# Forty pairs of modulation columns: from products and sums on ScalarE and GpSimd to matrix multiplications on TensorE

## The chip, the cores and the metric

One core of a Trainium2 chip runs the whole kernel. The metric is the device time of one execution in microseconds (us). Three executions of the kernel before took 1823.52, 1839.77 and 1840.11 us, median 1839.77 us.

## The reference, cut to what matters

The model has two layers over 512 latent tokens and 256 context tokens of width 1024. Each layer takes six vectors of 1024 values (shift, scale and gate for the mixer and for the MLP) from one conditioning vector:

```python
s_lat = jax.nn.silu(c)[:, None, :]
for layer in range(DEPTH):                       # DEPTH = 2
    mod = jnp.split(s_lat @ mod_w[layer] + mod_b[layer], 6, axis=-1)   # mod_w: (2, 1024, 6144)
    h = modulate(rms_norm(x, norm_mix_pre[layer]), mod[0], mod[1])
    # mixer: layer 0 = DeltaNet + attention, layer 1 = short convolution
    x = x + mod[2] * rms_norm(y, norm_mix_post[layer])
    h = modulate(rms_norm(x, norm_ffn_pre[layer]), mod[3], mod[4])
    x = x + mod[5] * rms_norm(conv_ffn(h, ...), norm_ffn_post[layer])
```

The product of the vector with `mod_w` is a matrix-vector product with 2 x 6144 output columns. Only `mod[0]` and `mod[1]` of layer 0 are needed before the mixer; the other ten vectors are needed after the attention.

## The kernel before

**The data.** The conditioning vector lies as `cvec`, 128 partitions by 8 chunks (k). A "modulation pair" is a block of 256 columns of `mod_w`: 1 MB, laid in SBUF as 128 partitions by 8 chunks by 256 columns. There are 48 pairs. The first 8 are multiplied by TensorE at the start with `cvec` as the stationary operand (L543) and are not touched here. The 40 later ones, j = 0 to 39, go through six buffers `mod_raw_c` (`MSLOTS`) and end as 80 columns (128 values, one in each partition) in PSUM bank 7, from where VectorE adds the bias after the attention.

**The path of a later pair before.** SyncE's queue loads pair j when pair j-6 has been counted in `mod_done` (`load_mod_pair`, L357). ScalarE multiplies the eight chunks by the eight scalars of `cvec`, in place, eight activations (`products`, L1079, recorded as L1082). GpSimd adds the eight chunks in three halving steps, in place (`mod_half`, recorded as L1888). TensorE then sums over the partitions with two matrix multiplications for a pair: each takes 128 columns of the sum as the stationary operand and a single column of ones as the moving one (`mod_column`, L487).

**The order.** There is no planner: every engine runs its list in order, and semaphores tie them. The DeltaNet has six chunk steps s (`NT`) of seven levels l (`LEVELS`), two directions d in each, four heads. A level l >= 1 is: VectorE makes masked blocks `bl` (L1582); TensorE multiplies Z = bl x t (L689) for both directions; ScalarE copies Z out (`zs`, L1174); TensorE makes dT and dU (L710, L715); VectorE subtracts them into `tu` (L1593). At level 0 there is no Z; TensorE waits there for `bl` made by GpSimd and `bv` made by VectorE (L701, L704). Between the Z of both directions and the first dT stands the call `mod_columns(...)`, in every level, with the pairs that are due.

Pair j < 24 is due at level number `MOD_LEVEL[j]` = 7*(j//4) + 2*(j%4), so four pairs in seven levels: ScalarE at this number, GpSimd two and three levels later, TensorE four levels later. The other 16 pairs are due in the attention, which runs through 32 blocks i (8 heads by 4 query tiles): TensorE multiplies scores (L801, L802), transposes the probabilities of block i-2 (L775), multiplies a third of the values of an earlier head in three blocks of four (L786 to L788), then calls `mod_columns`. VectorE and ScalarE form the softmax and split each transposed block in a high and a low part. Pair j is due at block 7*(j-24)//4: ScalarE there, TensorE three blocks later, GpSimd in between.

fp32 matrix multiplications are recorded twice: one instruction in the code is two weight loads and two multiplications in the trace, here called passes. The 80 multiplications of L487 are 160 passes. Transposes, and the fp32r multiplications of split operands, are one pass.

Of the kernel before, what the change touches and what calls it, by code (L numbers as in the profile page):

```python
# [12 lines left out]
P = 128  # L13
# [39 lines left out]
def hybrid_trunk(nc, A, out):  # L53
    ctx = ExitStack()
    with ctx:
# [107 lines left out]
        def bank(b, n=512, o=0):  # L163
            return PS[:, b * 512 + o:b * 512 + o + n]
# [3 lines left out]
        def sem(name):  # L168
            if name not in sems:
                sems[name] = ctx.enter_context(nc.semaphore(name))  # L170
            return sems[name]
# [15 lines left out]

        PAIRS = MODS - 8
        DN_PAIRS = 24

        def acc_c(j):

            return 3 * (j + 1)

        def landed(j):

            return 16 * (j // MSLOTS + 1)
# [261 lines left out]
        def _(pe):  # L459
# [22 lines left out]
                        if k == KC - 1 and names[r]:  # L482
                            i.then_inc(sem(names[r]), 1)

            def mod_column(m, acc):

                mm(bank(7, 1, 16 + m), acc, ones[:, 0:1], start=True, stop=True).then_inc(sem("mod_done"), 1)  # L487

            def sum_columns(sq, idx, n, first, last):

                for j in range(n // P):
# [137 lines left out]
                item_rows(e)  # L629
            def mod_columns(pairs):  # L630
                for j in pairs:
                    pe.wait_ge(sem("mod_acc"), acc_c(j))
                    for part in range(2):
                        mod_column(16 + 2 * j + part, mraw_c[j % MSLOTS][:, 0, part * P:(part + 1) * P])

            def gate_rows(s):

# [12 lines left out]
            for s in range(NT):  # L650
# [30 lines left out]
                for l in range(LEVELS):  # L681
                    for d in range(2):
                        T, q = DT[d], (s * LEVELS + l) * 2 + d
                        if l == 0:
                            continue
                        pe.wait_ge(sem("Bl"), q + 1)
                        pe.wait_ge(sem("T"), q - 1)
                        for h in range(HEADS):
                            i = mm(bank(3 * d, P, h * P), T["bl"][:, h, :], T["tu"][:, h, :], start=True, stop=True)  # L689
                        i.then_inc(sem("Z"), 1)  # L690
                    mod_columns(mod_at(s * LEVELS + l, 4))
                    for d in range(2):
                        T, q, b0 = DT[d], (s * LEVELS + l) * 2 + d, 3 * d
                        if l == 0:
                            pe.wait_ge(sem("Bl"), q + 1)
                            pe.wait_ge(sem("TU0"), 2 * s + d + 1)
                            if CHUNK_ORDER[d][s] >= NTC:
                                pe.wait_ge(sem("egr"), 2 * s + d - 3)
                            pe.wait_ge(sem("bv"), 2 * s + d + 1)
                            for h in range(HEADS):  # L700
                                i = mm(bank(b0 + 1, P, h * P), T["bl"][:, h, :], T["tu"][:, h, :], start=True, stop=True)  # L701
                            i.then_inc(sem("dT"), 1)
                            for h in range(HEADS):
                                i = mm(bank(b0 + 2, P, h * P), T["tu"][:, 4 + h, :], T["bl"][:, h, :], start=True, stop=True)  # L704
                            i.then_inc(sem("dU"), 1)
                            continue
                        pe.wait_ge(sem("Zs"), z_count(s, l, d))
                        pe.wait_ge(sem("U"), u_count(s, l - 1, d))
                        for h in range(HEADS):
                            i = mm(bank(b0 + 1, P, h * P), T["tu"][:, 4 + h, :], T["zs"][:, h, :], start=True, stop=True)  # L710
                        i.then_inc(sem("dT"), 1)
                        if l == LEVELS - 1:
                            continue
                        for h in range(HEADS):
                            i = mm(bank(b0 + 2, P, h * P), T["zs"][:, h, :], T["tu"][:, 4 + h, :], start=True, stop=True)  # L715
                        i.then_inc(sem("dU"), 1)
                    if s == 0 and l < 6:
                        att_rows(l)
# [16 lines left out]
                for d in range(2):  # L735
# [9 lines left out]
                    for h in range(HEADS):  # L745
                        i = mm(bank(3 * d + 2, P, h * P), T["kd"][:, h, :], T["kbvn"][:, h, :], start=True, stop=True)
                    i.then_inc(sem("Sp"), 1)
            for q in range(LEVELS * NT, LEVELS * NT + 5):
                mod_columns(mod_at(q, 4))

            pe.wait_ge(sem("S"), 2 * NT)
            for n in range(NT):
# [41 lines left out]
            for i in range(A_HEADS * NQ + NQ + 1):  # L794
                if i < A_HEADS * NQ:
                    hh, qt = divmod(i, NQ)
                    t, half = hh % 4, hh // 4
                    r = slice(HD * half, HD * (half + 1))
                    pe.wait_ge(sem("expd"), cnt(i - 1))
                    b = 2 * (i % 2)  # L800
                    mm(bank(b), aq[r, t, qt * P:(qt + 1) * P], ak[r, 0:512], start=True, stop=True)  # L801
                    mm(bank(b + 1, CTX), aq[r, t, qt * P:(qt + 1) * P], ak[r, 512:768], start=True, stop=True).then_inc(sem("sc"), 1)  # L802
                if 2 <= i < A_HEADS * NQ + 2:
                    turn(i - 2)
                if i >= 6 and (i - 6) % NQ < 3:
                    values((i - 6) // NQ, (i - 6) % NQ)
                mod_columns(mod_block(i, 3))


            tcol = lambda r: (lambda w, k: w[slot[0]][:, k, r * P:(r + 1) * P])  # L810
# [228 lines left out]
        def _(act):  # L1039
# [36 lines left out]
            h_high(0, hc_hi, CTX, lambda c: modv[:, 0, c, 1:2])  # L1076
            h_high(1, h_hi, SEQ, lambda c: modv[:, 0, c, 0:1])

            def products(slot):  # L1079

                for k in range(KC):
                    i = nc.scalar.activation(slot[:, k, :], slot[:, k, :], ACT.Copy, scale=cvec[:, k, 0:1])  # L1082
                i.then_inc(sem("mod_prod"), 1)


            def square(e):
                t, n = items[e]
                if e >= 2:
# [74 lines left out]
            for s in range(NT):  # L1163
# [6 lines left out]
                for l in range(LEVELS):  # L1170
                    for d in range(2 if l else 0):
                        T = DT[d]
                        act.wait_ge(sem("Z"), z_count(s, l, d))
                        nc.scalar.activation(T["zs"][:, :, :].rearrange("p h t -> p (h t)"), bank(3 * d), ACT.Copy).then_inc(sem("Zs"), 1)  # L1174
                    for j in mod_at(s * LEVELS + l, 0):
                        act.wait_ge(sem(f"mod_in{j % MSLOTS}"), landed(j))
                        products(mraw_c[j % MSLOTS])
                for d in range(2):
                    T, k = DT[d], 2 * s + d
                    act.wait_ge(sem("WT"), k + 1)  # L1180
# [36 lines left out]
            for i in range(A_HEADS * NQ + NQ + 2):  # L1217
                if 2 <= i < A_HEADS * NQ + 2:
                    turn_hi(i - 2)
                if i < A_HEADS * NQ:  # L1220
                    act.wait_ge(sem("mx"), 2 * i + 2)
                    act.wait_ge(sem("Ptr"), cnt(i - 2))
                    nc.scalar.activation(prob[i % 3][:, :], bank(2 * (i % 2), ALL), ACT.Exp, scale=HD ** -0.5,
                                         bias=stat[:, 32 + i:33 + i], accum_out=stat[:, 64 + i:65 + i]).then_inc(sem("expd"), 1)
                if i >= 9 and (i - 9) % NQ == 0:
                    head_hi((i - 9) // NQ)
                for j in mod_block(i, 0):
                    act.wait_ge(sem(f"mod_in{j % MSLOTS}"), landed(j))
                    products(mraw_c[j % MSLOTS])
                if i == A_HEADS * NQ:  # L1230
                    act.wait_ge(sem("mod_done"), 2 * PAIRS)
                    split_hi(U_WOUT, 0)
                    split_hi(U_WOUT + 1, 1)
# [636 lines left out]
        def _(pool):  # L1870
# [10 lines left out]
                        i = G.tensor_tensor(t4[2][:, 0:n], t4[2][:, 0:n], t4[c % 2][:, 0:n], ALU.add)  # L1881
                    i.then_inc(sem("sqadd"), 1)

            def mod_add(n, dst, a, b):

                if n % 3:
                    pool.wait_ge(sem("mod_acc"), n)
                G.tensor_tensor(dst, a, b, ALU.add).then_inc(sem("mod_acc"), 1)  # L1888

            def mod_half(n, slot):  # L1890
                w = 4 >> (n % 3)
                mod_add(n, slot[:, 0:w, :], slot[:, 0:w, :], slot[:, w:2 * w, :])

            post_squares(0)
            post_squares(1)
            pool.wait_ge(sem("h"), KC)
            pool.wait_ge(sem("rope_in"), 32)

            def mod_parts(j, parts):
                pool.wait_ge(sem("mod_prod"), j + 1)  # L1900
                for part in parts:
                    mod_half(3 * j + part, mraw_c[j % MSLOTS])

            def mod_level(q):

                for lag, parts in ((3, (1, 2)), (2, (0,))):
                    for j in mod_at(q, lag):
                        mod_parts(j, parts)

            pool.wait_ge(sem("dn_ready"), 1)  # L1910
            for s in range(NT):
# [8 lines left out]
                for l in range(LEVELS):  # L1920
# [13 lines left out]
                    if s == 0 and 1 <= l < 6:  # L1934
                        pool.wait_ge(sem("shuf"), 2 * l - 1)
                        G.tensor_tensor(rope_tile(l - 1), rope_tile(l - 1), cosT[:, :], ALU.mult).then_inc(sem("rcos"), 1)
                    mod_level(s * LEVELS + l)
            for q in range(LEVELS * NT, LEVELS * NT + 4):
                mod_level(q)
            for j in range(DN_PAIRS, PAIRS):  # L1940
                mod_parts(j, (0, 1, 2))
            for j in range(4):
                for t in range(1, ACC):
                    pool.wait_ge(sem("ysq"), KC * j + t + 1)
# [50 lines left out]
```

## Time and profile before

| | us | share |
|---|---|---|
| profiled execution, own time | 1840.32 | |
| its span (first to last instruction) | 1838.2 | |
| TensorE multiplications busy | 1732.5 | 94% |
| TensorE weight loads busy | 1447.7 | 79% |
| VectorE busy | 984.0 | 54% |
| ScalarE busy | 704.0 | 38% |
| GpSimd busy | 324.2 | 18% |
| ScalarE's products (L1082, 320) | 131.7 | |
| GpSimd's sums (L1888, 120) | 189.4 | |

The DeltaNet levels run until 632 us of the span, the attention from 647 to 804 us, the rest (output projection, MLPs, short convolution) until the end. "PEclk" is the clock that TensorE was granted, as a share of 2.4 GHz; 0.50 is 1.2 GHz, its other level. A busy share of TensorE's multiplications counts overlapping records once and says little of how full it is; the starts of its weight loads (PEld), one behind the other, show how fast it goes.

### The profile page before, as it was taken

To read this page: it belongs to the slowest core of one execution; us is meant where nothing else is said; L and a number is where in the kernel's file an instruction comes from. 1 tells how busy PE (TensorE), PEld (TensorE's weight loads), DVE (VectorE), ACT (ScalarE), POOL (GpSimd) and SP (SyncE) were. 2 spreads that over 40 slices of the span, in tenths; PEclk is the share of its full clock that TensorE was granted. 3 is DMA by queue.
4 is the path that set the end of the run, shared out by engine and by line. 5 is a ranking of instruction groups with operands and counts; after the bars stand their busy time and mean duration, and the time that the engine had idled before them with its cause. 6 is when DMAs were issued, how large, how long until landed. Compare 5 with 4: busy or idle time off the path is not lost.

```text
span 1838.2 us, 22745 instructions
## 1 busy us (share of the span) xinstructions
PE 1732.5 (94%) x9143; PEld 1447.7 (79%) x9143; DVE 984.0 (54%) x1248; ACT 704.0 (38%) x1056; POOL 324.2 (18%) x227
## 2 busy tenths in 40 slices
PE   6899997989988999889999999999999999999998
PEld 3688887889988955657788888887888788888886
DVE  2633267777787565757644443446446744444222
ACT  2433433444444476834333332223223244433321
POOL 3000014543464345504000000110002100000000
PEclk9899998999999966989999999998999899999999
DMA  9213141212221323132232223230322122233221
GB/s 323 65 47 92 23 150 46 70 47 70 93 69 47 115 76 107 47 92 70 72 110 93 91 91 103 86 109 28 110 95 93 65 92 92 91 100 100 86 83 66
DMA packets 160942, 161.14 MB, mean 88 GB/s; under 512 B 11367, under 2 KB 159192, under 8 KB 160728
## 3 DMA queue, kind: packets, MB, share of 16 engines
q1 hardware_dynamic: 160856, 159.92, 27.4%
q8 instruction: 63, 1.03, 0.2%
q14 instruction: 23, 0.19, 0.0%
HBM read 157.81 MB, written 2.10 MB: 87 GB/s over the span
## 4 chain that ended last, share of the span: by engine, by line
PE 84%; DVE 8%; ACT 4%; issue 2%; POOL 1%; DMA 1%; SPq 0%; DVEq 0%; ACTq 0%; POOLq 0%
PE ps L467 17%; PE ps L468 17%; PE ps L469 17%; PE ps L710 3%; PE ps L689 3%; PE ps L715 3%; ACT mod_raw_c L1082 2%; PE ps L543 2%; PE ps L801 1%; PE ps L775 1%; PE ps L818 1%; PE ps L820 1%; PE ps L840 1%; PE ps L819 1%; DVE w_lo L1364 1%
## 5 line engine op out<-in xcount | busy, mean ns | idle before, releaser
L1364 DVE TENSOR_TENSOR w_lo<-w_raw,w_hi 128x2048 fp32r<-128x2048 f32 x100 | 229.0, 2291 | 513.9 <-ACT w_hi L1044 513.9
L467 PE MATMUL ps<-h_hi,w_hi 128*128 128x512 f32 x968 | 379.0, 392 | 0.4 <-DVE w_lo L1364 0.4
L468 PE MATMUL ps<-h_lo,w_hi 128*128 128x512 f32 x968 | 378.3, 391 | 0.0
L469 PE MATMUL ps<-h_hi,w_lo 128*128 128x512 f32 x968 | 377.9, 390 | 0.0
L1044 ACT ACTIVATE w_hi<-w_raw 128x2048 fp32r<-128x2048 f32 x100 | 191.1, 1913 | 337.7 <-PE ps L469 307.3
L1888 POOL TENSOR_TENSOR mod_raw_c<-mod_raw_c 128x1024 f32<-128x1024 f32 (+2 forms) x120 | 189.4, 1581 | 145.3 <-ACT mod_raw_c L1082 138.3
L467 PEld LDWEIGHTS ps<-h_hi,w_hi 128*128 128x128 f32 x968 | 182.5, 188 | 38.6 <-DVE w_lo L1364 0.8
L469 PEld LDWEIGHTS ps<-h_hi,w_lo 128*128 128x128 f32 x968 | 182.6, 189 | 38.0
L468 PEld LDWEIGHTS ps<-h_lo,w_hi 128*128 128x128 f32 x968 | 182.6, 189 | 37.6
L467 PE MATMUL ps<-mid_hi,w_hi 128*128 128x512 f32 x338 | 133.0, 394 | 0.0
L469 PE MATMUL ps<-mid_hi,w_lo 128*128 128x512 f32 x338 | 131.9, 390 | 0.0
L1948 POOL TENSOR_TENSOR sum_acc_y<-sum_acc_y,sum_y 128x512 f32<-128x512 f32 x18 | 27.0, 1502 | 594.2 <-ACT sum_y L1248 594.2
L1082 ACT ACTIVATE mod_raw_c<-mod_raw_c,cvec 128x256 f32<-128x256 f32 x320 | 131.7, 499 | 0.0
L468 PE MATMUL ps<-mid_lo,w_hi 128*128 128x512 f32 x338 | 131.7, 390 | 0.0
L1593 DVE TENSOR_TENSOR dn_tu<-dn_tu,ps 128x512 f32<-128x512 f32 x156 | 102.6, 682 | 40.5 <-PE ps L710 29.6
L1174 ACT ACTIVATE dn_zs<-ps 128x512 f32<-128x512 f32 x72 | 43.0, 597 | 160.0 <-PE ps L689 160.0
L1582 DVE TENSOR_TENSOR dn_bl<-dn_ta,const 128x512 f32<-128x512 f32 x72 | 97.0, 1381 | 4.5 <-PE ps L689 3.9
L689 PE MATMUL ps<-dn_tu,dn_bl 128*128 128x128 f32 x576 | 77.6, 285 | 12.8 <-DVE dn_bl L1582 11.3
L689 PEld LDWEIGHTS ps<-dn_tu,dn_bl 128*128 128x128 f32 x576 | 70.2, 196 | 17.8 <-DVE dn_bl L1582 14.3
L710 PE MATMUL ps<-dn_zs,dn_tu 128*128 128x128 f32 x576 | 84.0, 295 | 0.0
L710 PEld LDWEIGHTS ps<-dn_zs,dn_tu 128*128 128x128 f32 x576 | 76.0, 207 | 0.0
L1948 POOL TENSOR_TENSOR tmp<-tmp,tmp 128x512 f32<-128x512 f32 x6 | 7.8, 1293 | 380.2 <-ACT tmp L1244 380.2
(328 smaller groups left out, 2821.6 us busy)
## 6 DMA issues: line engine op xcount, KB each, us to landing
w_raw<-in_ffn_w_up SPq DMA_DIRECT2D x44, 1024.0 KB, 5.1
mod_raw_c<-in_mod_w SPq DMA_DIRECT2D x40, 1024.0 KB, 5.2
w_raw<-in_ffn_w_down SPq DMA_DIRECT2D x16, 896.0 KB, 4.9
w_raw<-in_sc_w_in SPq DMA_DIRECT2D x12, 1024.0 KB, 5.2
w_raw<-in_hyb_w_in SPq DMA_DIRECT2D x9, 1024.0 KB, 5.3
mod_raw_a<-in_mod_w SPq DMA_DIRECT2D x8, 1024.0 KB, 13.3
w_raw<-in_ffn_w_down SPq DMA_DIRECT2D x8, 1024.0 KB, 5.1
w_raw<-in_sc_w_out SPq DMA_DIRECT2D x4, 1024.0 KB, 5.3
```

The source lines that it names most:

```text
L467: mm(dst, hi, xh[:, k0 + k, :], start=first and k == 0, stop=False)
L468: mm(dst, hi, xl[:, k0 + k, :], start=False, stop=False)
L469: i = mm(dst, lo, xh[:, k0 + k, :], start=False, stop=last and k == nk - 1)
L689: i = mm(bank(3 * d, P, h * P), T["bl"][:, h, :], T["tu"][:, h, :], start=True, stop=True)
L710: i = mm(bank(b0 + 1, P, h * P), T["tu"][:, 4 + h, :], T["zs"][:, h, :], start=True, stop=True)
L715: i = mm(bank(b0 + 2, P, h * P), T["zs"][:, h, :], T["tu"][:, 4 + h, :], start=True, stop=True)
L1044: nc.scalar.activation(whi[s][:, :], raw[s][:, :], ACT.Copy).then_inc(sem("w_hi"), 1)
L1082: i = nc.scalar.activation(slot[:, k, :], slot[:, k, :], ACT.Copy, scale=cvec[:, k, 0:1])
L1364: V.tensor_tensor(wlo[s][:, :], raw[s][:, :], f32(whi[s][:, :]), ALU.subtract).then_inc(sem("w_lo"), 1)
L1582: V.tensor_tensor(T["bl"][:, :, :], T["ta"][:, :, :], bh(C(C_LVL + LEVELS * d + l), HEADS), ALU.mult).then_inc(sem("Bl"), 1)
L1593: V.tensor_tensor(t, t, bank(3 * d + 1 + o // HEADS), ALU.subtract).then_inc(sem(name), 1)
L1888: G.tensor_tensor(dst, a, b, ALU.add).then_inc(sem("mod_acc"), 1)
```

## The change

TensorE takes the raw pair itself. For each of the two halves of a pair it makes eight multiplications, one for each chunk k, with 128 raw columns as the stationary operand and the column k of `cvec` as the moving one, and accumulates the eight in one PSUM column. ScalarE's products and GpSimd's sums are gone. The call comes one level (or one block) after the pair's due number instead of four (or three), and waits for the load instead of the sum. Slots, loads and the bank are as before.

```diff
             def mod_columns(pairs):
                 for j in pairs:
-                    pe.wait_ge(sem("mod_acc"), acc_c(j))
+                    slot = mraw_c[j % MSLOTS]
+                    pe.wait_ge(sem(f"mod_in{j % MSLOTS}"), landed(j))
                     for part in range(2):
-                        mod_column(16 + 2 * j + part, mraw_c[j % MSLOTS][:, 0, part * P:(part + 1) * P])
+                        for k in range(KC):
+                            i = mm(bank(7, 1, 32 + 2 * j + part), slot[:, k, part * P:(part + 1) * P], cvec[:, k, 0:1],
+                                   start=k == 0, stop=k == KC - 1)
+                        i.then_inc(sem("mod_done"), 1)
...
-                    mod_columns(mod_at(s * LEVELS + l, 4))
+                    mod_columns(mod_at(s * LEVELS + l, 1))
...
-            for q in range(LEVELS * NT, LEVELS * NT + 5):
-                mod_columns(mod_at(q, 4))
+            for q in range(LEVELS * NT, LEVELS * NT + 2):
+                mod_columns(mod_at(q, 1))
...
-                mod_columns(mod_block(i, 3))
+                mod_columns(mod_block(i, 1))
...
-            def products(slot):
-                for k in range(KC):
-                    i = nc.scalar.activation(slot[:, k, :], slot[:, k, :], ACT.Copy, scale=cvec[:, k, 0:1])
-                i.then_inc(sem("mod_prod"), 1)
...
-                    for j in mod_at(s * LEVELS + l, 0):
-                        act.wait_ge(sem(f"mod_in{j % MSLOTS}"), landed(j))
-                        products(mraw_c[j % MSLOTS])
...
-                    mod_level(s * LEVELS + l)
-            for q in range(LEVELS * NT, LEVELS * NT + 4):
-                mod_level(q)
-            for j in range(DN_PAIRS, PAIRS):
-                mod_parts(j, (0, 1, 2))
```

(The same calls go from ScalarE's attention loop, and the helpers `mod_column`, `mod_add`, `mod_half`, `mod_parts`, `mod_level` and `acc_c` go with their uses.)

## Rows read from the trace of the kernel before

**Rows 1.** The page, 40 slices of the span: granted clock in tenths.

```profile
PEclk9899998999999966989999999998999899999999
```

**Rows 2.** Busy time in three stretches: us, each engine, PEclk, DMA share, GB/s.

```profile
286.00:632.00 346.00, 311.14 (x2562) 301.71 (x2562) 260.29 (x354) 147.58 (x303) 164.50 (x110) 0.96 0.21 68
647.00:804.00 157.00, 141.74 (x510) 92.12 (x510) 102.70 (x171) 112.03 (x233) 72.56 (x48) 0.77 0.27 81
690.00:735.00 45.00, 40.62 (x121) 26.82 (x119) 24.62 (x39) 28.37 (x61) 23.89 (x17) 0.63 0.32 104
```

**Rows 3.** The page: ScalarE's products and the loads of the pairs; then line L487 alone.

```profile
L1082 ACT ACTIVATE mod_raw_c<-mod_raw_c,cvec 128x256 f32<-128x256 f32 x320 | 131.7, 499 | 0.0
mod_raw_c<-in_mod_w SPq DMA_DIRECT2D x40, 1024.0 KB, 5.2
L487 PEld LDWEIGHTS ps<-const,mod_raw_c x160: 187/192/338, 293.2 to 789.6; 128*128 128x128 f32 x160
```

**Rows 4.** Order of time in two levels: start, us, engine, line, operation.

```profile
413.26 5.17 POOL L1888 TENSOR_TENSOR mod_raw_c<-mod_raw_c 128x1024 f32<-128x1024 f32 x3 [2.66 <-ACT mod_raw_c L1082]
413.92 3.92 DVE L1582 TENSOR_TENSOR dn_bl<-dn_ta,const 128x512 f32<-128x512 f32 x2 [0.20 <-PE ps L689]
414.50 0.53 PEld L487 LDWEIGHTS ps<-const,mod_raw_c 128*128 128x128 f32 x4
414.95 0.97 PEld L710 LDWEIGHTS ps<-dn_zs,dn_tu 128*128 128x128 f32 x8
...
420.15 1.49 DVE L1582 TENSOR_TENSOR dn_bl<-dn_ta,const 128x512 f32<-128x512 f32 x2
```

**Rows 5.** The chain that ended last, by line: 286 to 632 us, then 632 to 806.

```profile
by line: PE ps L710 16.4%; PE ps L689 16.0%; PE ps L715 14.1%; ACT mod_raw_c L1082 4.6%; issue 4.5%; DVE dn_bl L1582 3.7%; PE ps L729 3.5%; PE ps L701 3.0%; PE ps L704 2.6%; PE ps L731 2.6%; PE ps L487 2.3%; POOL mod_raw_c L1888 2.3%; DVE d
by line: PE ps L801 14.4%; ACT mod_raw_c L1082 12.9%; PE ps L775 12.7%; issue 6.7%; PE ps L802 5.9%; PE ps L786 5.3%; ACT prob L1223 5.0%; PE ps L787 4.9%; PE ps L788 4.7%; DVE PTl L1668 3.7%; PE ps L764 3.5%; DVE prob L1662 3.1%; ACT PTh L
```

**Rows 6.** What TensorE's weight loads waited for, 286 to 632: us, times, longest.

```profile
PEld ps L689 <- DVE dn_bl L1582: 13.7, 11, 3.0
PEld ps L487 <- POOL mod_raw_c L1888: 9.4, 2, 4.9
PEld ps L679 <- DVE dn_tb L1566: 6.0, 4, 1.5
PEld ps L701 <- issue: 5.7, 4, 1.4
```

**Rows 7.** TensorE around runs of single-column passes: in order of time, then stretches with PEclk.

```profile
633.99 4.28 PE L759 MATMUL ps<-const,tmp 128*128 128x1 f32 x32
...
1442.65 1.84 PE L840 MATMUL ps<-const,sum_acc_z 128*128 128x1 f32 x8
1444.36 1.84 PE L840 MATMUL ps<-const,sum_z 128*128 128x1 f32 x8
...
633.40:636.80 3.40, 3.40 (x32) 1.00 0.96 307
636.80:643.60 6.80, 6.08 (x29) 0.50 0.48 155
1438.90:1442.30 3.40, 2.87 (x25) 1.00 0.00 0
1442.40:1449.10 6.70, 6.70 (x29) 0.50 0.01 2
```

**Rows 8.** Weight loads of one attention block at the full clock, in order of time.

```profile
747.13 0.30 PEld L801 LDWEIGHTS ps<-ak,aq 64*128 64x128 f32 x2 [0.35 <-issue]
...
748.61 0.64 PEld L775 LDWEIGHTS ps<-const,prob 128*128 128x128 f32 x6 [0.33 <-issue]
749.22 0.19 PEld L786 LDWEIGHTS ps<-PTh,Vh 128*128 128x128 f32 x1
...
750.50 0.65 PEld L487 LDWEIGHTS ps<-const,mod_raw_c 128*128 128x128 f32 x4
751.16 0.30 PEld L801 LDWEIGHTS ps<-ak,aq 64*128 64x128 f32 x2
```

More of the change, by code:

```diff
@@ L189, in hybrid_trunk @@
         DN_PAIRS = 24
-        def acc_c(j):
-            return 3 * (j + 1)
         def landed(j):
@@ L483, in mm3_first @@
                             i.then_inc(sem(names[r]), 1)
-            def mod_column(m, acc):
-                mm(bank(7, 1, 16 + m), acc, ones[:, 0:1], start=True, stop=True).then_inc(sem("mod_done"), 1)
             def sum_columns(sq, idx, n, first, last):
@@ L1226, in _ @@
                     head_hi((i - 9) // NQ)
-                for j in mod_block(i, 0):
-                    act.wait_ge(sem(f"mod_in{j % MSLOTS}"), landed(j))
-                    products(mraw_c[j % MSLOTS])
                 if i == A_HEADS * NQ:
@@ L1882, in post_squares @@
                     i.then_inc(sem("sqadd"), 1)
[L1884 to L1892, printed above, removed]
             post_squares(0)
@@ L1897, in _ @@
             pool.wait_ge(sem("rope_in"), 32)
[L1899 to L1908, printed above, removed]
             pool.wait_ge(sem("dn_ready"), 1)
```

## The prediction

> **What bounds the kernel now.** I read the page first: TensorE is the busy engine, and its granted clock shows one dark place, two slices at 0.6 in the attention [rows 1]. The table of stretches puts numbers to it: the DeltaNet levels run at 0.96 of full clock, the attention at 0.77, one piece of it at 0.63 [rows 2]. Then the order of time inside a level: L710 begins 0.45 us after the four weight loads of L487 began, and nothing of TensorE's stands idle between them [rows 4]. The levels are bound by TensorE's weight loads. The chain of waits comes last, and shows what the change could free: ScalarE's products hold 4.6% of it in the levels and 12.9% in the attention, GpSimd's sums 2.3% in the levels [rows 5].
>
> **What is added.** A pair takes 16 multiplications instead of 2, so 32 passes instead of 4; for 40 pairs 1280 passes instead of 160 [rows 3]. What does a pass with one moving column cost? Four take 0.45 us at full clock (414.50 to 414.95) [rows 4], so 0.1125 us; eight take 1.71 us at half clock (1442.65 to 1444.36) [rows 7], so 0.214 us. The weight load sets this pace, the narrow moving operand saves nothing. A pair is then 32 x 0.1125 = 3.6 us at full clock, 6.8 us at half. The bounds of a pass are these two clocks; both are measured on the same kind of pass.
>
> **DeltaNet levels, at full clock.** 24 pairs x (3.6 - 0.45) = +76 us. Each block stands between Z and the first dT, with all later work of TensorE queued behind it; ScalarE's copy of Z is hidden beneath it, and then ScalarE and VectorE wait too. Against it stand pauses of the weight loads that go or are covered. The wait for the sums, 9.4 us, goes whole. The wait for VectorE's masks, 13.7 us: two masks took 3.92 us while GpSimd was adding and 1.49 us while it was not [rows 4], so I take back 10 of it. At level 0 a block now stands where TensorE paused for `bl` and `bv`: 5.7 us is covered. Of the wait of L679, 6.0 us, a third (2 us) [rows 6]. Sum 27 us; bounds 9 and 35 (all four rows). The levels gain +49 us at an unchanged clock.
>
> **The clock.** This term decides the rest. The row before a fall says what the engine did: in 633.40 to 636.80 TensorE was busy for all 3.40 us with 32 passes, most of them the single-column passes of L759, and the clock then stood at 0.50 for 6.8 us. In 1438.90 to 1442.30, busy 2.87 us and nearly all L840's single columns, it fell again and stood at 0.50 for 6.7 us [rows 7]. So a dense run of single-column passes does not hold the clock, though the engine is never idle. The change puts 40 such runs of 3.6 us into the kernel.
>
> A page of the Trainium skill speaks the other way. "TensorE: Matmul & The Clock Gate", part 1 and the section "Why this matters for your kernels", says that the gate follows how busy TensorE has been, and advises against idle gaps between bursts; by it a TensorE that has fewer pauses would keep its clock, which is the first rival below. Rows 7 differ: busy was full and the clock fell.
>
> In the levels dense 128-column work follows each block, so a spell of half clock should be short. Its cost is half its length. Bounds: none, and 6.8 us a block as in rows 7; I take half of that row, 3.4 us, since dense work stands right before the block and right behind it, which rows 7 have on neither side or on one alone. So 24 x 1.7 = 41 us lost. The levels lose (1 - 0.96) x 346 = 14 us already [rows 2], mostly behind pauses that go. Net +27 us; bounds -14 and 24 x 3.4 - 14 = +68. Levels together: +49 + 27 = +76 us.
>
> **Attention.** Work of TensorE at full clock from one block [rows 8]: scores 1.48 us (747.13 to 748.61), transposes 0.61, values 1.28 (749.22 to 750.50), the old columns 0.66. For 32 blocks 32 x 2.09 = 67, values in 24 of them 31, the new pairs 16 x (3.6 + 0.2 of switching) = 61: 159 us. Today the stage lasts 157 us [rows 2] with 108 us of such work, stretched by half clock and by waits behind ScalarE's products (12.9% of 174 us, 22 us). Those waits go; the blocks cover what is left. So TensorE's clock sets the stage: time = 159 / clock. It cannot be under 159 us, and not over 318. The stage has 0.77 now and 0.63 where it is worst [rows 2], and that with 64 single-column passes in it; now there are 512, a run every block or two, and a spell at half clock has no time to end before the next run. I take 0.67, nearer to 0.63: 237 us, +80 us. Bounds: 159/0.77 = 206 (+49) and 318 (+161).
>
> **What costs nothing.** The loads: a pair's slot is free when pair j-6 is done, some twelve levels or ten blocks earlier, and the load takes 5.2 us [rows 3]; SyncE's queue holds nothing else then. If that cover went, TensorE would wait out 5.2 us a pair. ScalarE's 131.7 us of products [rows 3] and the sums free engines that do not set the pace, beyond the waits counted. The last pair ends two blocks earlier in the attention; the weights behind it wait for the attention's end anyway.
>
> **Sum.** 1840.3 (the profiled execution, 0.5 us above the median of the runs) + 76 + 80 = 1996; I say 1995 us.
>
> **Rivals.**
> *The blocks keep the clock.* If weight loads count as activity, the fuller TensorE falls less. Levels +49 - 14 = +35; attention 159 us and a third of today's 22 us of waits, +9 or 10: 1885 us. With the clocks as they are now it is +49 and +49: 1938 us. For it: a few passes of L487 at a time do no harm today (0.96). Against: rows 7. Chance 0.12.
> *Half clock throughout.* The spells behind a block last 6.8 us in the levels and the attention never recovers: +49 + 68 + 161 = 2118 us. For it: at 690 to 735 us there is little full clock [rows 2]. Against: that stage did recover twice. Chance 0.06.
> *Faster: the chain is freed and the passes slip in.* Products and sums are 4.6% + 2.3% of 346 us and 12.9% of 174 us of the chain, 46 us [rows 5]. If the added passes lay wholly beside other work, in TensorE's place between Z and dT where it waits for ScalarE's copy, the time would be 1840 - 46 = 1794 us. It decides from the point where an added block costs under 46 / 40 = 1.15 us. Against: the added 28 passes are 3.15 us, and L710 follows L487 without a pause [rows 4]. Chance 0.02.
>
> **Numbers.** My case has 0.80, its own range 1930 to 2060. The range of 1915 to 2055 us adds part of the first rival and leaves out 2 in 10. A measurement can tell about 1%, 18 us, from no change. Faster 0.02, within 1% 0.02, slower 0.96.
>
> **What would show it.** The new line should have 1280 weight loads, 0.11 us apart at full clock and 0.21 at half, and no wait for its load. ScalarE's busy time should fall by some 130 us and GpSimd's by the 189 us of its sums; VectorE's masks (L1582) should be near 0.7 us each. The levels' 346 us should be near 420, the attention's 157 near 237, with PEclk about 0.67 there and about 0.90 in the levels. I am wrong in the clock if PEclk stays over 0.95 in the levels, and wrong in the mechanism if L710 starts less than 2 us after a block begins.

## The result, and the profile after

The changed kernel takes 1995.41 us (median of 4 runs, 1987.11 to 2005.96) against 1836.76 us before: ratio 1.0881, 95% interval 1.0797 to 1.0966. The forecast was 1995 us. The profiled execution has a span of 1987.0 us, 148.8 us longer than the 1838.2 us before. The profiled execution before was the slowest of its kernel in this measurement, and some 10 us above the medians of 1827 to 1831 us that the same kernel has in the experiments below: where a stage is compared with the stage before, up to 10 us in all can come from that.

The page, busy time and clock in 40 slices of the span:

```profile
PE 1914.2 (96%) x10263; PEld 1623.3 (82%) x10263; DVE 934.9 (47%) x1248; ACT 578.7 (29%) x736; POOL 133.5 (7%) x107
PEclk9899989989989866667999999999999999999999
```

ScalarE lost 125.3 us of busy time and GpSimd 190.7; TensorE gained 181.7 us of recorded busy time, and the dark place of [rows 1] has grown from two slices to five and spread small dips before it.

From here on a stage is measured in every kernel in the same way. The levels run from the first weight load of the chunk's first product (L659 before) to that of L764 before; the attention runs from the first scores to the first split of the output weights. For the kernel before, then the changed one (us, then busy PE, PEld, DVE, ACT, POOL, then PEclk, DMA share, GB/s):

```profile
255.30:639.00 383.70, 346.05 (x2882) 334.55 (x2880) 289.86 (x401) 164.80 (x335) 175.39 (x117) 0.96 0.21 69
647.10:802.40 155.30, 141.62 (x510) 92.12 (x510) 101.00 (x170) 110.41 (x233) 72.56 (x48) 0.77 0.27 82
```

```profile
255.30:709.90 454.60, 438.08 (x3553) 431.97 (x3551) 248.53 (x401) 89.34 (x143) 57.23 (x45) 0.91 0.18 59
718.40:955.80 237.40, 235.18 (x958) 174.44 (x958) 92.83 (x169) 60.45 (x105) 0.00 (x0) 0.65 0.18 54
```

Levels +70.9 us, attention +82.1, the rest within a few us. In the attention TensorE's record has hardly a gap left (235.18 of 237.40 us), and its clock is lower than before. The new line in the changed kernel (durations in ns: min, median, max), and the masks of the levels, first before and then after:

```profile
L628 PEld LDWEIGHTS ps<-cvec,mod_raw_c x1280: 187/192/338, 267.8 to 933.6; 128*128 128x128 f32 x183
```

```profile
L1582 DVE TENSOR_TENSOR dn_bl<-dn_ta,const x72: 677/1362/2842, 265.2 to 613.7; 128x512 f32<-128x512 f32 x72
```

```profile
L1565 DVE TENSOR_TENSOR dn_bl<-dn_ta,const x72: 676/692/1107, 265.2 to 676.5; 128x512 f32<-128x512 f32 x72
```

1280 passes, as counted; and the masks took half the time. That GpSimd's adding beside them is what slowed them is shown by two experiments below: without the sums alone the median mask takes 692 ns too, without the products alone, the sums kept, 1098 ns. One run of the new passes and what follows it, in order of time (weight loads: start, us), then TensorE over three stretches (busy, PEclk):

```profile
414.02 3.65 PEld L628 LDWEIGHTS ps<-cvec,mod_raw_c 128*128 128x128 f32 x32
417.60 0.97 PEld L706 LDWEIGHTS ps<-dn_zs,dn_tu 128*128 128x128 f32 x8
418.49 1.56 PEld L711 LDWEIGHTS ps<-dn_tu,dn_zs 128*128 128x128 f32 x8
419.93 1.83 PEld L706 LDWEIGHTS ps<-dn_zs,dn_tu 128*128 128x128 f32 x8
421.64 1.24 PEld L711 LDWEIGHTS ps<-dn_tu,dn_zs 128*128 128x128 f32 x8
```

```profile
415.40:418.70 3.30, 3.30 (x31) 1.00 0.00 0
418.80:422.10 3.30, 3.30 (x18) 0.50 0.95 308
786.00:821.00 35.00, 35.00 (x117) 0.50 0.27 89
```

The run takes 3.58 us (414.02 to 417.60), eleven weight loads later the clock falls, and eight loads of L706 take 1.71 us (419.93 to 421.64) where they took 0.89 from 417.60 on. TensorE was busy in every moment of the first stretch. The third stretch lies in the attention: 35 us, busy for all of them, at half clock throughout.

### The profile page after: what moved, and what is told of

Its sections match the earlier page's. It is cut to its first block, busy times and chain, and to the rows that moved or that the text cites. A ratio compares the mean times of both kernels' runs of the same rounds, so it can differ in the third digit from the quotient of the medians.

```text
span 1987.0 us, 24521 instructions
## 1 busy us (share of the span) xinstructions
PE 1914.2 (96%) x10263; PEld 1623.3 (82%) x10263; DVE 934.9 (47%) x1248; ACT 578.7 (29%) x736; POOL 133.5 (7%) x107
## 4 chain that ended last, share of the span: by engine, by line
PE 91%; DVE 5%; issue 1%; DMA 1%; ACT 1%; SPq 0%; POOL 0%; DVEq 0%; ACTq 0%; POOLq 0%
PE ps L463 16%; PE ps L464 16%; PE ps L465 16%; PE ps L628 8%; PE ps L706 4%; PE ps L685 3%; PE ps L711 3%; PE ps L797 3%; PE ps L771 2%; PE ps L535 1%; PE ps L798 1%; PE ps L814 1%; PE ps L815 1%; PE ps L816 1%; DVE w_lo L1347 1%
## 5 line engine op out<-in xcount | busy, mean ns | idle before, releaser
L628 PEld LDWEIGHTS ps<-cvec,mod_raw_c 128*128 128x128 f32 x1280 | 172.8, 219 | 1.8 <-issue 0.7
L1576 DVE TENSOR_TENSOR dn_tu<-dn_tu,ps 128x512 f32<-128x512 f32 x156 | 106.8, 687 | 141.6 <-PE ps L706 105.3
L628 PE MATMUL ps<-cvec,mod_raw_c 128*128 128x1 f32 x1280 | 170.6, 267 | 0.0
L706 PE MATMUL ps<-dn_zs,dn_tu 128*128 128x128 f32 x576 | 93.8, 317 | 0.0
L1663 DVE TENSOR_REDUCE att_stat<-ps 128x1 f32<-128x768 f32 x32 | 30.6, 958 | 128.8 <-PE ps L798 128.8
L706 PEld LDWEIGHTS ps<-dn_zs,dn_tu 128*128 128x128 f32 x576 | 85.6, 229 | 0.0
L685 PE MATMUL ps<-dn_tu,dn_bl 128*128 128x128 f32 x576 | 71.3, 277 | 7.3 <-DVE dn_bl L1565 7.3
L1195 ACT ACTIVATE PTh<-ps 128x768 fp32r<-128x768 f32 x32 | 26.0, 812 | 173.3 <-PE ps L771 173.3
```

The costliest lines, as they stand in the source:

```text
L628: i = mm(bank(7, 1, 32 + 2 * j + part), slot[:, k, part * P:(part + 1) * P], cvec[:, k, 0:1], start=k == 0, stop=k == KC - 1)
L1576: V.tensor_tensor(t, t, bank(3 * d + 1 + o // HEADS), ALU.subtract).then_inc(sem(name), 1)
```

## The experiments

Two theories stood against each other: that the loss is the added passes at the pace of the weight loads plus half clock brought on by runs of single-column passes; and that the clock, or the time, comes from something else in the new order. "Levels" and "attention" are the two stages above, of the profiled execution. The diffs are shortened to the lines that matter, with "..." where code is left out.

**The same passes with a wide moving operand.**

```diff
-  mm(bank(7, 1, 32 + 2 * j + part), slot[:, k, part * P:(part + 1) * P], cvec[:, k, 0:1], ...)
+  mm(bank(7, P, 32 + 2 * j + part), slot[:, k, part * P:(part + 1) * P], cvec[:, k, 0:1].to_broadcast([P, P]), ...)
```

> The changed kernel with a moving operand of 128 equal columns instead of one: the same 1280 weight loads in the same places, each followed by a 128-column multiplication (127 of the columns land in PSUM columns that later pairs overwrite). Theory (passes at the weight load's pace, plus half clock brought on by runs of single-column passes): the passes keep their 0.11 us, the clock stays up, the levels take some 420 us instead of the changed kernel's 455, the attention some 166 to 180 instead of 237; 1885 us, at most 1910. Rival (the falls of the clock come from anything else in the new order, such as the place of the blocks): as the changed kernel, 1995 us. Rival (a wider multiplication costs more per pass): over 2000 us.

Measured: 1883.60 us, ratio to before 1.0295 (1.0269 to 1.0321). The two stages, and one run with the loads around it:

```profile
254.70:673.00 418.30, 401.79 (x3554) 395.68 (x3552) 248.50 (x401) 89.37 (x143) 57.20 (x45) 1.00 0.20 64
681.10:848.20 167.10, 162.11 (x958) 123.68 (x958) 90.79 (x169) 60.71 (x105) 0.00 (x0) 0.99 0.25 76
```

```profile
416.40 3.65 PEld L628 LDWEIGHTS ps<-cvec,mod_raw_c 128*128 128x128 f32 x32
419.98 0.97 PEld L706 LDWEIGHTS ps<-dn_zs,dn_tu 128*128 128x128 f32 x8
420.87 0.97 PEld L711 LDWEIGHTS ps<-dn_tu,dn_zs 128*128 128x128 f32 x8
421.76 0.97 PEld L706 LDWEIGHTS ps<-dn_zs,dn_tu 128*128 128x128 f32 x8
```

128 times the columns, the same 3.58 us for a run, and 112 us less in all. Weight loads, places and waits are those of the changed kernel; only the width of the moving operand differs. The clock is 1.00 and 0.99. So the narrow operand is shown to be the cause of the difference, and against a wide one it costs 1995.41 - 1883.60 = 112 us (106 between the two profiled executions). Widths between 1 and 128 were not tried. Part of the 112 us is not half clock that the added passes brought on, but half clock that the wide ones ended; the next experiment shows it.

**The removal alone: 4 passes a pair, no products, no sums.** Seven eighths of the modulation product are left out.

```diff
-                        for k in range(KC):
-  ... start=k == 0, stop=k == KC - 1)
+                        for k in range(1):
+  ... start=k == 0, stop=k == 0)
```

> The changed kernel with one chunk of eight in each half of a pair: 4 passes a pair as before, and neither products nor sums (seven eighths of the modulation product are left out). It measures the removal alone. Theory: the levels lose 27 us of waits and the attention 22 us or more against the kernel before: 1790 us (1770 to 1800). Rival (the freed engines were worth nothing): 1837 us. The difference from 1995 us is then the price of 28 further passes a pair, 40 times: 205 us by the theory, of which 126 are passes at full clock and the rest is clock.

Measured: 1780.57 us, 0.9727 (0.9703 to 0.9752), some 50 us under the kernel before.

```profile
255.40:605.40 350.00, 327.47 (x2882) 320.80 (x2881) 246.97 (x401) 89.42 (x143) 57.30 (x45) 1.00 0.24 76
613.50:742.60 129.10, 124.05 (x510) 80.54 (x510) 91.16 (x170) 61.09 (x105) 0.00 (x0) 0.88 0.34 98
```

Levels -33.7 us, attention -26.2; that is 59.9 us where the medians differ by 50, for the reason given with the result. The idea of the change was sound on its gaining side. Much of the gain is clock: 0.96 to 1.00 of 383.7 us is 15 us in the levels, and 0.77 to 0.88 some 20 us in the attention. Here is TensorE in the removal's attention, first its start and then the rest:

```profile
613.60:644.00 30.40, 30.40 (x74) 18.03 (x75) 18.28 (x35) 11.66 (x20) 0.00 (x0) 0.50 0.32 104
644.00:742.60 98.60, 93.57 (x438) 62.41 (x436) 72.79 (x136) 49.33 (x86) 0.00 (x0) 1.00 0.34 96
```

TensorE pauses for 2.1 us between the levels and the attention, the clock falls as the attention begins, and the attention's own work then goes on at half clock for 30.4 us, with only three runs of four single-column passes in it. The kernel below that has no pair in the attention at all shows the same (662 to 689 us at 0.50). The wide kernel pauses and falls there too (0.73 and 0.50 from 683 us on), but its clock is back at 687 us, inside its first wide run. So some 14 us of the attention's half clock (0.12 of 129.1 us, less what the wide kernel still loses) is there without any added pass. What keeps the clock down in those 30.4 us is open.

From here to the wide kernel, which adds 28 passes a pair, is 1883.60 - 1780.57 = 103 us, where 1120 passes of 0.1125 us make 126. Of the 23 us between them, those 14 us of clock are the larger part; the rest lay in pauses, such as the one at level 0.

**Runs of half the length.**

```diff
-  mod_columns(mod_at(s * LEVELS + l, 1))            # both halves of the pair, 32 passes
+  for part in (1, 0):
+      mod_columns(mod_at(s * LEVELS + l, 1 + part), part)    # one half, 16 passes; the same in the attention
```

> The changed kernel with each pair's two halves apart: the first one level (or attention block) after the due number, the second one later, so that runs of 16 single-column passes stand between dense work instead of runs of 32. Same passes. Theory (it is the length of the run against the dense work around it that costs the clock): in the levels the clock stays up, PEclk over 0.97, levels near 425 us; in the attention, where dense work is thinner, the clock still falls: 225 us; 1955 us in all. Rival (only the number of single-column passes counts): 1995 us.

Measured: 1972.39 us, 1.0766 (1.0740 to 1.0791).

```profile
255.10:685.30 430.20, 414.10 (x3554) 408.08 (x3552) 248.87 (x401) 89.40 (x143) 57.27 (x45) 0.96 0.19 62
693.70:941.40 247.70, 246.36 (x958) 190.56 (x958) 93.66 (x170) 60.43 (x105) 0.00 (x0) 0.61 0.17 51
```

A miss in part, 17 us over the 1955 expected. The levels gained 24.4 us on the changed kernel and took 430.2 us where 425 was expected, but the clock was 0.96, not over 0.97. The attention did not fall to 225 us: it rose by 10.3, to 247.7, at a clock of 0.61. In the attention the halves left hardly a block without single-column passes, and shorter runs may help only where enough dense work stands between them; that fits both stages, but no run here separates it from other reasons. So neither the number of passes alone nor the length of a run alone decides.

**One stage at a time.** In the levels alone, then in the attention alone:

```diff
-                    mod_columns(mod_at(s * LEVELS + l, 4))
+                    mod_new(mod_at(s * LEVELS + l, 1))      # mod_new: the changed mod_columns
-                    for j in mod_at(s * LEVELS + l, 0): ... products(...)
-                    mod_level(s * LEVELS + l)
...
```

> The change in the DeltaNet levels alone; the attention's 16 pairs keep products, sums and 4 passes. Theory (the two stages' losses stand by themselves): levels some 455 us, attention some 155 us: 1905 us. Rival (the attention's half clock is set off by what the levels leave behind): attention clearly over 165 us.

```diff
-                mod_columns(mod_block(i, 3))
+                mod_new(mod_block(i, 1))
-                for j in mod_block(i, 0): ... products(...)
-            for j in range(DN_PAIRS, PAIRS):
-                mod_parts(j, (0, 1, 2))
...
```

> The change in the attention alone; the 24 pairs of the levels keep products, sums and 4 passes. Theory: levels some 384 us, attention some 237 us with two thirds of it at half clock: 1915 us. Rival (losses do not add): under 1900 us.

Measured: 1918.49 us, 1.0502 (1.0479 to 1.0525), and 1914.60 us, 1.0481 (1.0460 to 1.0502). The stages of the first, then of the second:

```profile
254.70:719.20 464.50, 447.98 (x3554) 441.86 (x3553) 248.62 (x401) 89.43 (x143) 57.22 (x45) 0.89 0.17 56
727.60:877.90 150.30, 137.59 (x510) 89.98 (x510) 99.82 (x170) 110.48 (x233) 72.95 (x48) 0.78 0.28 84
```

```profile
254.50:638.30 383.80, 346.04 (x2882) 334.49 (x2880) 290.02 (x401) 165.00 (x335) 175.47 (x117) 0.96 0.21 68
646.40:879.10 232.70, 230.46 (x958) 171.30 (x958) 92.91 (x170) 60.55 (x105) 0.00 (x0) 0.67 0.18 55
```

The losses stand by themselves: 91 and 87 us over the 1827.51 us of the kernel before beside them, 178 together where the whole change lost 159, or 168 against the same 1827.51. The stage that was left as before looks as before (150.3 and 383.8 us). The changed levels came out 9.9 us longer than in the changed kernel at a clock of 0.89 instead of 0.91, with the same instructions, which is also most of the 13 us by which the first run missed its 1905: this much a stage's clock varies, and single readings of it are no finer.

**Which of the two removed parts was worth what.** Without GpSimd's sums (the sum over seven chunks is left out), then without ScalarE's products (the multiplication by the conditioning vector is left out):

```diff
-                    pe.wait_ge(sem("mod_acc"), acc_c(j))
+                    pe.wait_ge(sem("mod_prod"), j + 1)       # and GpSimd's mod_level, mod_parts calls go
```

> The kernel before without GpSimd's sums: TensorE takes chunk 0 of the products (the sum over the other seven chunks is left out). It splits the gain of the removal. Theory: the sums cost the levels the wait of L487 and the slow masks, so levels some 356 us against 384; the attention keeps its products and stays near 152; 1800 us. Rival (the products are what counts everywhere): over 1825 us.

```diff
-                    for j in mod_at(s * LEVELS + l, 0): ... products(...)      # and those in the attention
-                pool.wait_ge(sem("mod_prod"), j + 1)
+                pool.wait_ge(sem(f"mod_in{j % MSLOTS}"), landed(j))
```

> The kernel before without ScalarE's products: GpSimd sums the raw chunks as soon as they are loaded (the multiplication by the conditioning vector is left out). Theory: the products cost the attention, 155 us falls to some 131; the levels stay near 380; 1805 us. Rival (sums and products cost the same stage): attention over 145 us.

Measured: 1798.58 us, 0.9842 (0.9815 to 0.9869), and 1812.74 us, 0.9929 (0.9912 to 0.9945).

```profile
255.00:608.90 353.90, 329.34 (x2882) 320.75 (x2880) 247.00 (x401) 164.99 (x335) 57.34 (x45) 1.00 0.23 75
617.00:761.40 144.40, 130.36 (x510) 84.70 (x510) 91.96 (x170) 110.52 (x233) 0.00 (x0) 0.83 0.29 88
```

```profile
254.70:635.00 380.30, 343.82 (x2881) 333.78 (x2879) 282.92 (x401) 89.39 (x143) 196.80 (x131) 0.96 0.22 70
643.80:774.50 130.70, 123.05 (x510) 80.67 (x510) 97.38 (x169) 60.93 (x105) 45.19 (x30) 0.88 0.32 97
```

In the levels the sums were nearly all of the gain (29.8 of 33.7 us), in the attention the products (24.6 us). Without the sums the attention is 10.9 us shorter as well, where some 3 were expected; as the unchanged attention took 150.3 us in one run and 155.3 in another, only about half of that is certain. The second run took 8 us more than its 1805.

The levels show here why their clock was 0.96: without the sums it is 1.00, with them 0.96. Before, TensorE twice stood still for GpSimd's sum, and the clock was at half behind each pause. The first of the two (weight loads with the wait in brackets, then two stretches):

```profile
293.19 0.93 PEld L487 LDWEIGHTS ps<-const,mod_raw_c 128*128 128x128 f32 x4 [4.88 <-POOL mod_raw_c L1888]
294.00 1.83 PEld L710 LDWEIGHTS ps<-dn_zs,dn_tu 128*128 128x128 f32 x8
```

```profile
289.00:292.40 3.40, 0.00 (x0) 0.00 (x0) 3.40 (x4) 3.33 (x9) 3.32 (x3) 0.95 0.00 0
292.40:295.80 3.40, 2.60 (x12) 2.61 (x13) 1.29 (x2) 0.00 (x0) 0.74 (x1) 0.50 0.09 31
```

**The calls as late as before.**

```diff
-                    mod_columns(mod_at(s * LEVELS + l, 1))
+                    mod_columns(mod_at(s * LEVELS + l, 4))
-                mod_columns(mod_block(i, 1))
+                mod_columns(mod_block(i, 3))
```

> The changed kernel with its calls as late as before: four levels after the due number and three blocks after it in the attention. Same passes, runs of the same length. Theory: no block stands at level 0 any more, so the pause for the masks and values there is paid besides: 5 to 10 us more than the changed kernel, 2003 us. Rival (early calls make TensorE wait for loads or bring on falls of the clock): faster than the changed kernel by 10 us or more.

Measured: 1998.14 us, 1.0921 (1.0884 to 1.0958), not told apart from the changed kernel's 1.0881 (1.0797 to 1.0966). The levels are 8.9 us longer (463.5) and the attention takes 238.3. What its weight loads waited for at level 0 is a wait that the changed kernel does not show:

```profile
PEld ps L697 <- issue: 5.7, 4, 1.4
PEld ps L697 <- POOL dn_bl L1881: 1.2, 2, 1.0
```

So a block at level 0 does cover that pause; the rest of the 8.9 us is within the spread of the stage. Calls that come early are no cause of the loss.

**Versions that beat both kernels, by little.** They keep products and sums, and move pairs from the attention into the levels: all 40, one a level; all 40, fewer in the first chunk step; and 30, due at levels 0 to 4 of a chunk step from the second step on, with 10 in the attention.

```diff
-        DN_PAIRS = 24
-        MOD_LEVEL = [LEVELS * (j // 4) + 2 * (j % 4) for j in range(DN_PAIRS)]
+        DN_PAIRS = 40
+        MOD_LEVEL = list(range(DN_PAIRS))                                             # first
+        MOD_LEVEL = [0, 2, 4, 5, 6] + list(range(LEVELS, LEVELS * NT))                # second
...
+        DN_PAIRS = 30                                                                 # third
+        MOD_LEVEL = [0, 2, 4, 5, 6] + [LEVELS * (j // 5) + j % 5 for j in range(5, DN_PAIRS)]
+        # in the attention, pair j at block 3 * (j - DN_PAIRS)
```

> The kernel before, with all 40 pairs due in the levels, one a level, and none in the attention. Theory: the products no longer stand in ScalarE's way in the attention, which falls from 155 us to about 130; the levels get 16 more pairs, 7 us of TensorE's passes and more of the slow masks while GpSimd adds, 5 to 15 us; 1828 us (1810 to 1845), against 1837 before. Rival (GpSimd, with 4.7 us of sums in a level of 5.4, falls behind and TensorE waits for it): over 1860 us.

> The kernel before with all 40 pairs due in the levels, five in the first chunk step and one in every level after it. The version with one pair a level from the start waited 11.6 us for GpSimd in the first chunk step, where GpSimd also rotates queries and keys. Theory: most of that wait goes, the rest stays as there (attention some 121 us): 1815 us, 0.99 of the kernel before. Rival (the last pairs end too late, and TensorE waits for GpSimd after the levels): 1824 us or more.

> The kernel before with 30 pairs due in the levels (five in each chunk step, from the second step on at its levels 0 to 4) and 10 in the attention, one in three blocks. GpSimd then adds in levels 2 to 7 and has next to nothing to add while VectorE makes the masks of levels 1 and 2. Theory (two thirds of what all 40 pairs in the levels cost there is the wait for masks slowed by GpSimd's adding): the wait of L689 for the masks falls from 16.6 us towards 8, levels some 375 us against 395; the attention with 10 pairs of products some 136 us; 1808 us. Rival (the masks wait for something else): levels over 388 us, 1825 us.

Measured: 1824.01 us, 0.9970 (0.9944 to 0.9995); 1819.17 us, 0.9942 (0.9924 to 0.9960); 1818.94 us, 0.9934 (0.9909 to 0.9959). The stages of the second, then of the third:

```profile
256.60:652.00 395.40, 356.59 (x2945) 345.84 (x2945) 294.93 (x401) 215.86 (x463) 253.30 (x165) 0.94 0.30 96
659.80:783.10 123.30, 116.47 (x446) 69.76 (x446) 91.05 (x169) 61.07 (x105) 0.00 (x0) 0.89 0.00 1
```

```profile
254.80:638.20 383.40, 346.86 (x2905) 335.84 (x2904) 298.98 (x401) 184.97 (x383) 206.22 (x135) 0.96 0.27 85
646.60:782.50 135.90, 126.30 (x486) 79.58 (x486) 96.24 (x169) 91.65 (x184) 45.47 (x30) 0.85 0.16 45
```

Both are 0.6 to 0.7% faster than before, and not told apart from each other; the first gains 0.3%, hardly clear of noise. In the second the attention gains 32 us when it is rid of all pairs and the levels give back 12; of the 20 us between, 12 are seen in the medians. In the third, six more pairs cost the levels nothing, but the wait of L689 for the masks stayed at 13.7 us where 8 was expected, and the time missed the forecast by 11 us. The median mask took 1755 ns, against 1362 before: placing the sums away from the masks of levels 1 and 2 did not free the masks.

## Why the prediction was right

Its mechanism held: passes at the pace of the weight loads, less the waits that go, and half clock brought on by the narrow passes. That 1995 us was met to 0.4 us is luck. The changed kernel's own executions spread over 19 us, and between the profiled executions the sum of 156 us met 148.8: the levels +76 where +70.9 was measured, the attention +80 where +82.1, and the rest 4 us shorter.

**The passes.** 0.1125 us each at full clock, 32 a pair, was read from four passes of the kernel before and held for 1280: 3.58 us a run, 0.112 us a pass. Shown also by the wide kernel, where a 128 times wider operand took no longer. At an unchanged clock the prediction gave the levels +49 us; the wide kernel, whose clock is 1.00, has 418.3 us, 34.6 more than before, and with the 14 or 15 us that before lost to its clock (0.96) the +49 is met.

**The waits that go.** The sum of 27 us was right (26 us by the traces) by cancelling errors. The wait for the sums went whole, as did the pause at level 0. Of the wait for the masks, 13.7 us [rows 6], I took back 10 and 5.8 came back; of that of L675 (L679 before), 2 were expected and none came. After the change:

```profile
PEld ps L685 <- DVE dn_bl L1565: 7.9, 5, 1.6
PEld ps L675 <- DVE dn_tb L1549: 6.1, 4, 1.5
PEld ps L655 <- DVE S L1605: 2.3, 4, 0.8
```

That is 21 us of named waits. Smaller ones that no row of [rows 6] carried make up the difference: over the whole levels the waits of L689 for nothing that the profile shows fell from 3.2 to 0.9 us, that of L729 for ScalarE from 1.8 to none, that of L701 for GpSimd's `bl` from 2.5 to 1.3. The removal alone gave the levels 33.7 us, of which about 15 are their clock, from 0.96 to 1.00.

**The clock.** The step that decided the size was to follow [rows 7], where the clock fell behind a TensorE that was busy, and not the first rival. The removal alone, the wide kernel and the changed kernel give the whole ledger: levels 350.0, 418.3 and 454.6 us, attention 129.1, 167.1 and 237.4. So in the levels 36.3 us are clock, where 41 were predicted (the gross loss), a spell of about 3 us for each of 24 runs against the 3.4 taken. In the attention 70.3 us are clock, some 14 of them the spell at its start that the removal has too. The prediction took the stage as one mean clock and did not know of that spell. I took 0.67 there and it is 0.65; I took 159 us of work and 237.4 x 0.65 = 154 were there, so the two errors cancel. Nothing but the two neighbouring rows of before stood behind the 0.67, and the runs with these passes gave 0.61 to 0.67: this term was well placed, by a choice and not by a calculation, and 0.63 or 0.70 would have moved the total by 15 or 10 us.

**What costs nothing.** No wait for a load appears among the waits of L628, and the last slices of the span are as before.

**The rivals.** That the blocks keep the clock had 1885 us at full clock: the wide kernel, which makes just this true, measures 1883.60. That the time falls by 46 us when the added passes cost nothing: the removal alone measures 50 less (1830.41 to 1780.57). Both prices came out near and both conditions false; the second price is near partly by luck, as it was read from the chain of waits, and some 35 of the 59.9 us that the two stages lost are clock.

## What to carry to other kernels

A matrix-vector product on TensorE with the matrix as the stationary operand costs its weight loads, however narrow the moving operand is (here 0.112 us for each of the two passes of an fp32 block of 128x128, with 1 column or 128); count passes, and compare them with the pauses that they could fill. A dense run of single-column passes does not hold TensorE's clock, and what that costs is paid by everything behind it, the next run included, most in a stage that stands at half clock already. Widening the moving operand by a broadcast took that cost away. When two stages compete for the same side work, take the removal alone first: it says how much any scheme could gain (here 50 us), and where.

## What the runs showed of the hardware that was not expected

That the wide operand would win was expected only once its run was planned, and it is the result most worth knowing. A moving operand of 128 columns was faster for the kernel than one of a single column by 112 us, with 127 of its columns thrown away; a pass takes 0.112 us either way, and the clock is kept. Halving the length of the single-column runs helped the levels (430.2 against 454.6 us) and hurt the attention (247.7 against 237.4). And the clock can stay at its lower level for 35 us in which TensorE's record has no idle moment, and in the removal for 30.4 us of the attention's own work. The page "TensorE: Matmul & The Clock Gate" of the Trainium skill, section "Why this matters for your kernels", advises against idle gaps. In the levels before, the trace agrees: half clock stands behind a pause of 4.88 us. In the changed kernel it does not: before the fall at 418.8 us TensorE was busy for 3.30 of 3.30 us.
